# Expert stage of a hybrid block on one Trainium2 core: two 8 KB row gathers per pick become one 16 KB gather, and dots and sums run in the same turn

## The chip, the cores and the metric

The kernel runs on one core of a Trainium2 chip. The metric is the device time of one launch in microseconds (us), the median over several runs. One more execution was recorded by the hardware profiler; its trace is what the rows below come from.

## The reference, cut to what matters

A block of a hybrid model works on 256 tokens of width 2048 (with 256 context tokens for its recurrent branches): an RWKV-7 branch, a Mamba-2 branch, a merge, and last a feed-forward stage of experts (PEER). Only this last stage and the loads of its weights are touched by the change. All arrays are float32.

```
q = (tok @ wq).reshape(n, 8, 2, 128)                 # 8 heads, 2 half queries each
s = einsum('nhsd,hskd->nhsk', q, subkeys)            # scores against 128 keys per half
top_s, top_i = top_k(s, 16)
cand = top_s[:, :, 0, :, None] + top_s[:, :, 1, None, :]
best_s, best_j = top_k(cand.reshape(n, 8, 256), 16)
expert = i1 * 128 + i2                               # one of 16384 experts
gate = softmax(best_s)
act = gelu(einsum('nd,nhkd->nhk', x, u_tab[expert]))
out = einsum('nhk,nhkd->nd', gate * act, v_tab[expert])
x = x + g2x * rms_norm(out) * norm_post2
```

For each of the 256 tokens there are 8 heads with 16 experts each. Each expert costs a row of `peer_u` (2048 numbers, 8 KB), whose dot product with the token goes through a gelu, and a row of `peer_v` of the same size, which is added to the token's sum with the weight gate times gelu. That is 256 x 128 x 2 rows of 8 KB, 537 MB.

## The kernel before, in words

`hybrid_block` runs its stages one after the other: `rwkv`, `ssd`, and `tail`, which calls `mixing` (merge of the branches, `w_out`, the two norms) and `experts`. Each stage has one program per engine, written out in its order, and semaphores between them. The helper `Steps` counts named steps on one semaphore: `by(name, turn)` is the value after that step of that turn, `before(name, turn)` the one after the same step of the turn before.

Tokens lie on the 128 partitions, so 256 tokens are two tiles n = 0, 1. A **turn** is one head and one tile: 16 turns of 16 **picks**. One pick is one expert for each of the 128 tokens of the tile.

- `experts` first makes the queries on PE (`queries(h)`, L2448, 32 matmuls of 128x256 per head; `wq` comes in 2 MB pieces for one head, L1903, into the slot `w[:, 0]`) and the scores (`scoring(h)`, L2458). ACT copies both out of PSUM. Only when all eight heads are scored (`ready()` in `program`) does the loop over turns begin.
- DVE picks: `choose(i)` (L2259 to L2315, some 45 small instructions) finds the 16 best experts of head i for both tiles; `weigh(i)` (L2322 to L2326) makes the softmax gates after ACT's `exponent(i)` (L2386).
- GpSimd (POOL) gathers: `gather_u` (L2229) fetches 128 rows of 8 KB of `peer_u` into one of 4 buffers `ub`, `gather_v` (L2237) the same of `peer_v` into one of 4 buffers `vb`. A buffer is free again when the dot, or the matmuls, of the pick 4 earlier are done.
- DVE takes the dot (`dot`, L2334: one SCALAR_TENSOR_TENSOR of 128x2048 with a sum over the row) of each pick.
- After the 16 dots of a turn ACT takes one gelu (L2395), DVE multiplies by the gates (`coef`, L2356), ACT builds for each pick a diagonal matrix `diag` (L2401, 2 buffers), and PE adds diag times `vb` to the sums in PSUM (L2482: 4 matmuls of 128x512 per pick, 8 in the profile's count).
- So the two halves of a pick are a turn apart: `emit_v(v, ..., u, ...)` sums turn v while the dots of turn u = v + 1 are taken. POOL alternates strictly, one gather of v, one of u:

```
def emit_v(v, n, u, un, chosen):
    for k in range(TOPK):
        gather_v(v, n, k)
        if u is not None:
            gather_u(u, un, k)
```

- `choose` of the next head stands ahead of dot 4 in every other turn (`if k == 4 and chosen is not None`). DVE takes no dot while it runs.
- At the end, eight matmuls with zeros close the sums (L2489), ACT squares them (L2432), DVE scales and adds the residual (L2372 to L2379), and SP stores, tile 0 and then tile 1.

## Time and profile before

| what | us |
|---|---|
| median of 3 runs | 4236.61 (4233.58 to 4238.69) |
| the profiled execution | 4234.48 |
| its span, first to last instruction | 4232.7 |
| mean granted TensorE clock | 0.976 of full speed |
| PE busy | 3804.2 (90%) |
| DVE busy | 2031.0 (48%) |
| GpSimd busy | 778.2 (18%) |
| ACT busy | 729.5 (17%) |
| moved by DMA | 872.93 MB, 536.90 MB of them by the gathers |

The rows are read like this. Engines are PE (matmul), PEld (its weight load), DVE, ACT, POOL and SP; a group is named by its line of the kernel, and `out<-in` are its tensors. What stands in brackets or behind the last bar is the idle time of the engine just before, and what ended it. The share of busy time over the whole span mixes stages with different limits: the rwkv, ssd and mixing stages take the first 2790 us and are not touched.

### The profile page before, as it was taken

The page shows a single profiled execution, that of the slowest core. Times are in us where ns is not written, and L with a number is a line of the kernel's source. Part 1 is how long each engine was busy: PE and PEld are TensorE (multiplying, and loading weights), DVE is VectorE, ACT ScalarE, POOL GpSimd, SP SyncE. Part 2 cuts the span into 40 slices and gives each one's busy share as a digit, 9 for nine tenths or more (in the row PEclk, how much of TensorE's full clock was granted, in tenths as well). Part 3 has the DMA queues.
Part 4 walks back from the last instruction along what each step waited for, and adds up shares of the span by engine and source line. Part 5 has one row for each costly group of instructions (what it writes and reads, how often), then busy time and mean ns, then how long its engine had stood idle before and what let it go on. Part 6 is the DMA issues. An engine that isn't in the chain of part 4 may idle for free. (4 is left out here: it accounts for less than half of the span.)

```text
span 4232.7 us, 81256 instructions
## 1 busy us (share of the span) xinstructions
PE 3804.2 (90%) x35655; PEld 2313.7 (55%) x35655; DVE 2031.0 (48%) x3409; ACT 729.5 (17%) x1318; POOL 778.2 (18%) x755
## 2 busy tenths in 40 slices
PE   7999999999999989999999999988777777777777
PEld 3466666666666655666668888565223223322323
DVE  1355565556555547767770000035554554554541
ACT  2223222322233212221220000010110111111101
POOL 3000000001000100000010000004544444444431
PEclk9999999999999989999999999999999999999999
DMA  9211111111111117655663444437999999999996
GB/s 380 86 35 49 47 49 37 48 47 41 45 46 42 32 30 246 201 172 184 199 194 140 159 159 172 171 135 309 406 402 428 405 408 428 406 408 427 407 427 243
DMA packets 408824, 872.93 MB, mean 206 GB/s; under 512 B 16556, under 2 KB 250686, under 8 KB 341310
## 3 DMA queue, kind: packets, MB, share of 16 engines
q0 software_dynamic: 73728, 536.90, 30.5%
q1 hardware_dynamic: 243072, 284.82, 19.8%
q10 hardware_dynamic: 91710, 46.43, 3.8%
q8 instruction: 269, 4.41, 0.4%
q14 instruction: 45, 0.37, 0.0%
HBM read 863.87 MB, written 4.23 MB: 205 GB/s over the span
## 5 line engine op out<-in xcount | busy, mean ns | idle before, releaser
L2482 PE MATMUL ps<-w_slots,diag 128*128 128x512 f32 x2048 | 970.7, 622 | 302.6 <-DMA w_slots<-in_peer_v,ixv 264.5
L2482 PEld LDWEIGHTS ps<-w_slots,diag 128*128 128x128 f32 x2048 | 385.6, 197 | 887.5 <-issue 555.3
L979 PE MATMUL ps<-hT,w_slots 128*128 128x512 f32 (+1 forms) x1536 | 636.1, 542 | 3.1 <-PEq L230 2.2
L1719 PE MATMUL ps<-hT,w_slots 128*128 128x256 f32 (+1 forms) x1504 | 500.3, 486 | 6.5 <-PEq L655 4.9
L2334 DVE SCALAR_TENSOR_TENSOR junk<-w_slots,hT 128x2048 f32<-128x2048 f32 x128 | 293.4, 2292 | 290.3 <-DMA w_slots<-in_peer_u,ixu 289.6
L2334 DVE SCALAR_TENSOR_TENSOR junk<-ybT,hT 128x2048 f32<-128x2048 f32 x128 | 293.5, 2293 | 268.1 <-DMA ybT<-in_peer_u,ixu 266.3
L2237 POOL DMA_INDIRECT w_slots<-in_peer_v,ixv x256 | 293.7, 1147 | 550.0 <-PE ps L2482 497.3
L1719 PEld LDWEIGHTS ps<-hT,w_slots 128*128 128x128 f32 x1504 | 281.8, 191 | 173.3 <-issue 152.7
L979 PEld LDWEIGHTS ps<-hT,w_slots 128*128 128x128 f32 x1536 | 269.1, 191 | 179.7 <-issue 156.0
L2401 ACT ACTIVATE diag<-ident,coef 128x128 f32<-128x128 f32 x256 | 101.0, 400 | 1000.3 <-PE ps L2482 990.1
L695 POOL TENSOR_TENSOR bonus<-Kh 128x256 f32<-128x256 f32 x16 | 11.8, 735 | 1185.3 <-DVE Kh L916 1185.3
L2229 POOL DMA_INDIRECT ybT<-in_peer_u,ixu x128 | 170.1, 1329 | 196.2 <-PE ps L2482 81.5
L1603 DVE SCALAR_TENSOR_TENSOR w_slots<-w_slots,silu_c 128x512 f32<-128x512 f32 x240 | 193.9, 808 | 13.4 <-DVE w_slots L1603 0.9
L824 DVE SCALAR_TENSOR_TENSOR w_slots<-ps,em,w_slots 128x64 f32<-128x64 f32 x448 | 106.2, 278 | 195.0 <-PE ps L1078 195.0
L1986 PE MATMUL ps<-hT,w_slots 128*128 128x256 f32 x896 | 194.1, 379 | 0.3 <-PEq L1398 0.3
L1986 PEld LDWEIGHTS ps<-hT,w_slots 128*128 128x128 f32 x896 | 170.2, 190 | 23.8 <-issue 0.7
L844 DVE TENSOR_TENSOR w_slots<-ps,off 128x1024 f32<-128x1024 f32 x128 | 150.5, 1217 | 51.9 <-PE ps L1053 51.9
L2124 DVE TENSOR_TENSOR sga<-sga,ps 128x1024 f32<-128x1024 f32 x4 | 4.9, 1221 | 298.7 <-PE ps L1986 298.7
L2229 POOL DMA_INDIRECT w_slots<-in_peer_u,ixu x128 | 138.3, 1081 | 52.1 <-issue 42.7
L1078 PEld LDWEIGHTS ps<-w_slots 64*64 64x64 f32 x1792 | 71.1, 135 | 127.2 <-issue 109.4
L2448 PE MATMUL ps<-h2T,w_slots 128*128 128x256 f32 x512 | 115.7, 388 | 9.6 <-DMA w_slots<-in_peer_wq 8.4
L1439 POOL TENSOR_TENSOR xw<-xt,heads 128x256 f32<-128x256 f32 x48 | 27.7, 612 | 478.0 <-ACT xt L1498 478.0
(381 smaller groups left out, 4683.7 us busy)
## 6 DMA issues: line engine op xcount, KB each, us to landing
w_slots<-in_w_mod SPq DMA_DIRECT2D x128, 512.0 KB, 4.8
w_slots<-in_w_in SPq DMA_DIRECT2D x56, 1024.0 KB, 5.8
w_slots<-in_w_in ACTq DMA_DIRECT2D x44, 1024.0 KB, 6.9
w_mod_ring<-in_w_mod SPq DMA_DIRECT2D x16, 2048.0 KB, 12.6
w_slots<-in_w_in SPq DMA_DIRECT2D x7, 4096.0 KB, 13.8
w_slots<-in_w_branch_a SPq DMA_DIRECT2D x4, 4096.0 KB, 13.8
w_slots<-in_w_branch_b SPq DMA_DIRECT2D x4, 4096.0 KB, 13.8
w_slots<-in_w_out SPq DMA_DIRECT2D x4, 4096.0 KB, 12.7
```

The source lines that it names most:

```text
L824: stt(state(d, c), ps[:, 6, d * HEAD:(d + 1) * HEAD], em[:, z % 2, d, c:c + 1], state(d, c), ALU.mult, ALU.add).then_inc(*VD.did(f"c{j}_{d}"))
L844: tt(F[:, 2 * d:2 * d + 2, :, :], ps[:, 0:4, d * SEQ:(d + 1) * SEQ].rearrange("p r (h c) -> p h r c", h=2), off[:, l - 1, d, :].unsqueeze( ...
L979: last = mm(ps[:, 4, t0:TOK], w[m % 2][:, k, :], hT[:, k, t0:TOK], start=(k == 0), stop=(k == KC - 1))
L1603: stt(by_row[:, b, :], part, silu_c[:, k, 0:1], by_row[:, b, :], ALU.mult, ALU.add).then_inc(*VM.did(f"m{m}"))
L1719: last = mm(out, w[m % SLOTS_W][:, k, :], hT[:, k, t0:TOK], start=(k == 0), stop=(k == KC - 1))
L1986: last = mm(ps[:, bank + c // 2, (c % 2) * SEQ:(c % 2 + 1) * SEQ], slot[n][:, k, c * P:(c + 1) * P], rhs[:, k, :], start=(k == 0), stop=(k ...
L2229: nc.gpsimd.indirect_dma_start(ub[b], None, u_tab, bass.IndirectOffsetOnAxis(ap=ixu[:, n, k:k + 1], axis=0)).then_inc(u_in[b], 16)
L2237: nc.gpsimd.indirect_dma_start(vb[b], None, v_tab, bass.IndirectOffsetOnAxis(ap=ixv[:, n, k:k + 1], axis=0)).then_inc(v_in[b], 16)
L2334: nc.vector.scalar_tensor_tensor(junk[:, :], ub[k % NB], 1.0, h2_rows[:, n, :], ALU.mult, ALU.mult, accum_out=dots[:, k:k + 1]).then_inc(* ...
L2401: nc.scalar.activation(diag[:, k % 2, :], ident[:, :], ACT.Copy, scale=coef[:, k:k + 1]).then_inc(*DG.did(f"dg{k}"))
L2448: last = nc.tensor.matmul(ps[:, h % 2, s * SEQ:(s + 1) * SEQ], wq_at[h % 2][:, k, s * P:(s + 1) * P], h2T[:, k, :], start=(k == 0), stop=( ...
L2482: last = nc.tensor.matmul(ps[:, 4 * n + c, :], diag[:, k % 2, :], vb[k % NB][:, c * 512:(c + 1) * 512], start=False, stop=False)
```

## The change

1. The host lays `peer_u` and `peer_v` side by side in one table `peer_uv` whose rows have 4096 numbers, 16 KB. One gather per pick (L2222 of the new kernel) fetches both halves, 256 gathers of 128 rows in place of 512. There are 4 buffers `uv` of 16 KB per partition; they take the space of the 8 buffers of 8 KB.
2. Dots and sums belong to the same turn. For pick k DVE takes the dot, ACT the gelu of that one column, DVE builds the diagonal (`weighted`, one TENSOR_SCALAR of 128x128 with gelu and gate as its two scalars, 4 buffers), and PE runs the 4 matmuls. On DVE the diagonal of pick k - 1 stands behind the dot of pick k. The buffer is free when PE has done the pick (semaphore `x_pv`), and POOL waits for that before it issues the gather of pick k + 4.
3. `wq` is laid out by the host in 16 half heads, each contiguous, loaded as 1 MB pieces (`half_weights`). Heads 0 to 2 are done ahead of turn 0; eight half heads (heads 3 to 6) stand between the picks of turn 0 on PE, and head 7 behind it. The query banks move to PSUM 4 to 7, the sums of tile 0 have banks 0 to 3.
4. `choose` still stands ahead of dot 4 in the even turns; the gates of the head are made ahead of dot 8 of the same turn. The norm and store of tile 0 are done within the last turn.

```
-        ub = [part(spare, 0), part(spare, 1), part(w[:, 1, :], 2), part(w[:, 1, :], 3)]
-        vb = [part(w[:, 1, :], 0), part(w[:, 1, :], 1), part(w[:, 0, :], 0), part(w[:, 0, :], 1)]
+        uv = [flat(ybT), w[:, 1, 0:2 * D], w[:, 1, 2 * D:4 * D], w[:, 0, 0:2 * D]]
...
-        def program(emit_u, emit_v, engine, ready):
-            emit_u(0, 0)
-            ready()
-            with engine.Fori(0, PH - 1) as h:
-                emit_v(h * 2, 0, h * 2 + 1, 1, h + 1)
-                emit_v(h * 2 + 1, 1, h * 2 + 2, 0, None)
-            emit_v(TURNS - 2, 0, TURNS - 1, 1, None)
-            emit_v(TURNS - 1, 1, None, 0, None)
+        def program(turn, engine, after_first):
+            turn(0, 0, 1)
+            after_first()
+            turn(1, 1, None)
+            with engine.Fori(1, PH - 1) as h:
+                turn(h * 2, 0, h + 1)
+                turn(h * 2 + 1, 1, None)
+            turn(TURNS - 2, 0, None)
+            turn(TURNS - 1, 1, None)
... POOL
+                def turn(t_, n, chosen):
+                    wait_alone(pool, passed, *DU.before("ix", t_))
                     for k in range(TOPK):
-                        gather_v(v, n, k)
-                        if u is not None:
-                            gather_u(u, un, k)
+                        wait_alone(pool, passed, *(PV.by(f"v{k - NB}", t_) if k >= NB else PV.before(f"v{TOPK - NB + k}", t_)))
+                        nc.gpsimd.indirect_dma_start(uv[k % NB], None, uv_tab, bass.IndirectOffsetOnAxis(ap=ix[:, n, k:k + 1], axis=0)
+                                                     ).then_inc(uv_in[k % NB], 16)
... DVE
+                def weighted(t_, n, k):
+                    dve.wait_ge(*GE.by(f"g{k}", t_))
+                    dve.wait_ge(*(PV.by(f"v{k - NB}", t_) if k >= NB else PV.before(f"v{TOPK - NB + k}", t_)))
+                    if k == 0:
+                        dve.wait_ge(*DU.before("gt", t_))
+                    nc.vector.tensor_scalar(diag[:, k % NB, :], ident[:, :], acts[:, k:k + 1], gt[:, n, k:k + 1], ALU.mult,
+                                            ALU.mult).then_inc(*DG.did(f"dg{k}"))
+                def turn(t_, n, chosen):
+                    for k in range(TOPK):
+                        if k == 4 and chosen is not None:
+                            choose(chosen)
+                        if k == MID:
+                            if chosen is not None:
+                                weigh(chosen)
+                        dot(t_, n, k)
+                        if k:
+                            weighted(t_, n, k - 1)
+                        if final and k == MID + 2:
+                            normed(0)
+                    weighted(t_, n, TOPK - 1)
... PE
+                def turn(t_, n, chosen):
+                    for k in range(TOPK):
+                        pe.wait_ge(*DG.by(f"dg{k}", t_))
                         for c in range(4):
-                            last = nc.tensor.matmul(ps[:, 4 * n + c, :], diag[:, k % 2, :], vb[k % NB][:, c * 512:(c + 1) * 512],
+                            last = nc.tensor.matmul(ps[:, 4 * n + c, :], diag[:, k % NB, :], uv[k % NB][:, D + c * 512:D + (c + 1) * 512],
+                        if first and k % 2:
+                            m = 6 + k // 2
+                            half_query(m)
+                            if m % 2:
+                                scoring(m // 2 - 1)
```

What the written order makes of this is shown at three places. **DVE, two turns before the end, in the kernel before**: dots of one turn in a row (L2334), with nothing between them (`u_in` says that the gather of a `peer_u` row has landed).

```order
L2334 SCALAR_TENSOR_TENSOR junk,dots<-ybT,hT 128x2048 [waits x_du,u_in0]
L2334 SCALAR_TENSOR_TENSOR junk,dots<-ybT,hT 128x2048 [waits x_du,u_in1]
L2334 SCALAR_TENSOR_TENSOR junk,dots<-w_slots,hT 128x2048 [waits x_du,u_in2]
L2334 SCALAR_TENSOR_TENSOR junk,dots<-w_slots,hT 128x2048 [waits x_du,u_in3]
L2334 SCALAR_TENSOR_TENSOR junk,dots<-ybT,hT 128x2048 [waits x_du,u_in0]
```

**DVE at the same place in the changed kernel** (L2309 the dot, L2317 the diagonal; `uv_in` is the landing of a gather, `x_ge` the gelu, `x_pv` the matmuls of a pick).

```order
L2309 SCALAR_TENSOR_TENSOR junk,dots<-ybT,hT 128x2048 [waits x_du,uv_in0]
L2309 SCALAR_TENSOR_TENSOR junk,dots<-w_slots,hT 128x2048 [waits x_du,uv_in1]
L2317 TENSOR_SCALAR diag<-ident,acts,gt 128x128 [waits x_du,x_pv,x_ge]
L2309 SCALAR_TENSOR_TENSOR junk,dots<-w_slots,hT 128x2048 [waits x_du,uv_in2]
L2317 TENSOR_SCALAR diag<-ident,acts,gt 128x128 [waits x_pv,x_ge]
L2309 SCALAR_TENSOR_TENSOR junk,dots<-w_slots,hT 128x2048 [waits x_du,uv_in3]
L2317 TENSOR_SCALAR diag<-ident,acts,gt 128x128 [waits x_pv,x_ge]
```

The diagonal of pick 0 stands behind the dot of pick 1, which waits for the landing of gather 1, and so on. **PE in turn 0 of the changed kernel** (L2479 the sums of a pick, L2444 half a head of queries, L2458 scores).

```order
L2470 MATMUL ps<-g_rows,zero 128x512 x4
L2479 MATMUL ps<-ybT,diag 128x512 [waits x_dg]
L2479 MATMUL ps<-ybT,diag 128x512 x3
L2479 MATMUL ps<-w_slots,diag 128x512 [waits x_dg]
L2479 MATMUL ps<-w_slots,diag 128x512 x3
L2444 MATMUL ps<-h2T,w_slots 128x256 [waits q_cp,q_w0]
L2444 MATMUL ps<-h2T,w_slots 128x256 x15
L2479 MATMUL ps<-w_slots,diag 128x512 [waits x_dg]
L2479 MATMUL ps<-w_slots,diag 128x512 x3
```

Before, all 512 query matmuls (L2448) stood ahead of the first L2482; now the picks of turn 0 stand between those of heads 3 to 6. **POOL in the last turn**: the kernel before alternates the two gathers, each with its own semaphore; the changed one has one gather for a pick, which waits for PE alone.

```order
L2237 DMA w_slots<-in_peer_v,ixv 128x2048 [waits x_pv]
L2229 DMA ybT<-in_peer_u,ixu 128x2048 [waits x_du]
L2237 DMA w_slots<-in_peer_v,ixv 128x2048 [waits x_pv]
L2229 DMA w_slots<-in_peer_u,ixu 128x2048 [waits x_du]
```

```order
L2222 DMA ybT<-in_peer_uv,ix 128x4096 [waits x_pv]
L2222 DMA w_slots<-in_peer_uv,ix 128x4096 [waits x_pv] x3
```

A buffer of `u` used to come back with the dot (`x_du`); the joint buffer comes back with the matmuls (`x_pv`).

## Rows read from the trace of the kernel before

**Rows 1.** The page, the span in 40 slices: busy DMA in tenths, GB/s.
```profile
DMA  9211111111111117655663444437999999999996
GB/s 380 86 35 49 47 49 37 48 47 41 45 46 42 32 30 246 201 172 184 199 194 140 159 159 172 171 135 309 406 402 428 405 408 428 406 408 427 407 427 243
```

**Rows 2.** Stages: window, length, busy us (count) of five engines, PE clock, DMA share, GB/s.
```profile
2827.50:2925.30 97.80, 88.75 (x426) 77.82 (x425) 37.52 (x37) 10.44 (x16) 29.40 (x17) 0.95 0.70 271
2925.30:4147.50 1222.20, 919.65 (x1934) 363.13 (x1933) 663.75 (x987) 125.97 (x286) 561.52 (x484) 0.96 0.99 414
4147.50:4232.70 85.20, 63.76 (x144) 27.85 (x144) 9.62 (x6) 11.67 (x22) 11.24 (x12) 0.88 0.55 198
...
3400.00:3450.00 50.00, 37.42 (x82) 14.79 (x83) 28.91 (x74) 5.40 (x12) 20.02 (x19) 1.00 1.01 427
...
3165.00:3170.00 5.00, 3.77 (x9) 1.52 (x9) 2.30 (x2) 1.46 (x2) 2.41 (x2) 1.00 1.03 436
```

**Rows 3.** Timeline of PE, steady stretch: start us, us, line, count, idle before.
```profile
4122.23 3.67 PE L2482 MATMUL ps<-w_slots,diag 128*128 128x512 f32 x8 [1.19 <-DMA w_slots<-in_peer_v,ixv]
```

**Rows 4.** Timeline of POOL, the same stretch.
```profile
4126.72 0.96 POOL L2237 DMA_INDIRECT w_slots<-in_peer_v,ixv  x1 [2.66 <-PE ps L2482]
```

**Rows 5.** L2237 alone, 4147 to 4210 us, where the DMA queue is empty.
```profile
L2237 POOL DMA_INDIRECT w_slots<-in_peer_v,ixv x13: 936/936/962, 4146.3 to 4191.5; - x13
...
DMA to landing us min/median/max: 5.5/5.8/7.6
```

**Rows 6.** Timeline of DVE around one `choose` of the loop.
```profile
3102.13 2.29 DVE L2334 SCALAR_TENSOR_TENSOR junk<-ybT,hT 128x2048 f32<-128x2048 f32 x1 [2.63 <-DMA ybT<-in_peer_u,ixu]
...
3114.15 0.42 DVE L2259 COPY sc<-yaT 128x512 f32 x1
...
3129.98 2.29 DVE L2334 SCALAR_TENSOR_TENSOR junk<-ybT,hT 128x2048 f32<-128x2048 f32 x1 [0.21 <-DVE soft L2315]
3132.31 2.29 DVE L2334 SCALAR_TENSOR_TENSOR junk<-ybT,hT 128x2048 f32<-128x2048 f32 x1
...
3139.20 0.17 DVE L2346 COPY ixu<-idx 128x16 uint32 x1
```

**Rows 7.** Timeline of POOL beside the first dot of rows 6.
```profile
3103.26 1.97 POOL L2229 DMA_INDIRECT ybT<-in_peer_u,ixu  x1 [0.30 <-issue]
```

**Rows 8.** Timeline of PE behind three gaps.
```profile
3095.82 12.42 PE L2482 MATMUL ps<-w_slots,diag 128*128 128x512 f32 x24 [2.26 <-ACT diag L2401]
...
3143.93 5.44 PE L2482 MATMUL ps<-w_slots,diag 128*128 128x512 f32 x8 [6.32 <-DMA w_slots<-in_peer_v,ixv]
...
3155.00 3.67 PE L2482 MATMUL ps<-w_slots,diag 128*128 128x512 f32 x8 [1.61 <-DMA w_slots<-in_peer_v,ixv]
```

**Rows 9.** Windows (columns of rows 2) behind the gap that ends at 3095.82.
```profile
3096.40:3099.70 3.30, 3.30 (x5) 1.33 (x4) 2.30 (x2) 0.00 (x0) 0.26 (x1) 0.50 1.00 425
```

**Rows 10.** Chain that ended last, start of `experts`: start us, us, what.
```profile
2837.48 0.89 PE ps L2458 x8
2838.37 13.82 PE ps L2448 x64
```

**Rows 11.** Timeline of POOL: the first gather.
```profile
2827.50 1.23 POOL L2229 DMA_INDIRECT ybT<-in_peer_u,ixu  x1 [35.55 <-issue]
```

**Rows 12.** Chain that ended last, the end.
```profile
4147.51 56.90 PE ps L2482 x128
4204.41 6.88 PE ps L2489 x16
...
4211.39 1.97 ACT ybT L2432 x2
...
4219.91 3.81 DMA out_x<-w_slots
```

More of the change, by code:

```diff
@@ L2335, in dot @@
                                                    accum_out=dots[:, k:k + 1]).then_inc(*DU.did(f"dot{k}"))
-                def emit_u(u, n, chosen=None):
-                    fresh(DU)
-                    for k in range(TOPK):
-                        if k == 4 and chosen is not None:
-                            choose(chosen)
-                        if k == MID:
-                            if isinstance(u, int) and u == TURNS - 1:
-                                DU.skip("ixu")
-                            else:
-                                nc.vector.tensor_copy(ixu[:, 1 - n, :], idx[:, ds((u + 1) * TOPK, TOPK)]).then_inc(*DU.did("ixu"))
-                            wait_alone(dve, passed, *PV.before(f"v{TOPK - 1}", max(u - 1, 0) if isinstance(u, int) else u - 1))
-                            nc.vector.tensor_copy(ixv[:, n, :], idx[:, ds(u * TOPK, TOPK)]).then_inc(*DU.did("ixv"))
-                        dot(u, n, k)
@@ L2386, in exponent, with gelu @@
                     nc.scalar.activation(soft[:, :, :], soft[:, :, :], ACT.Exp).then_inc(*AC.did("exp"))
-                def emit_u(u, n):
-                    return
-                def emit_v(v, n, u, un, chosen):
+                def gelu(t_, k):
+                    act.wait_ge(*DU.by(f"dot{k}", t_))
+                    act.wait_ge(*DG.before(f"dg{k}", t_))
+                    nc.scalar.activation(acts[:, k:k + 1], dots[:, k:k + 1], ACT.Gelu).then_inc(*GE.did(f"g{k}"))
+                def turn(t_, n, chosen):
@@ L2392, in emit_v @@
                     fresh(GE)
-                    fresh(DG)
-                    act.wait_ge(*DU.by(f"dot{TOPK - 1}", v))
-                    nc.scalar.activation(acts[:, :], dots[:, :], ACT.Gelu).then_inc(*GE.did("gelu"))
-                    act.wait_ge(*DC.by("coef", v))
+                    first, final = (isinstance(t_, int) and t_ == at for at in (0, TURNS - 1))
                     for k in range(TOPK):
-                        if chosen is not None and k == 10:
+                        gelu(t_, k)
+                        if chosen is not None and k == 4:
@@ L2424, in _ @@
-                scoring(PH - 1)
-                program(emit_u, emit_v, act, lambda: None)
-                act.wait_ge(consts, 2)
-                act.wait_ge(*PV.by(f"v{TOPK - 1}", TURNS - 1))
-                act.wait_ge(opened, 2)
-                for n in range(2):
+                        if first and k in (5, 9, 13, 15):
+                            h = 3 + (5, 9, 13, 15).index(k)
+                            queries(h)
+                            scoring(h - 1)
+                        if final and k == 4:
+                            squared(0)
@@ L2464, in _ @@
                 queries(1)
[L2465 to L2482 removed]
+                queries(2)
@@ new lines, in _, with sums, turn @@
+                scoring(1)
+                def sums(m, first):
+                    for c in range(4):
+                        last = nc.tensor.matmul(ps[:, 4 * m + c, :], zero[:, :], g2_rows[:, c * 512:(c + 1) * 512], start=first, stop=not first)
+                    return last
+                def turn(t_, n, chosen):
+                    fresh(PV)
+                    first, final = (isinstance(t_, int) and t_ == at for at in (0, TURNS - 1))
+                    for k in range(TOPK):
+                        pe.wait_ge(*DG.by(f"dg{k}", t_))
+                        for c in range(4):
+                            last = nc.tensor.matmul(ps[:, 4 * n + c, :], diag[:, k % NB, :], uv[k % NB][:, D + c * 512:D + (c + 1) * 512],
@@ L2483, in emit_v @@
                                                     start=False, stop=False)
                         last.then_inc(*PV.did(f"v{k}"))
-                program(emit_u, emit_v, pe, lambda: None)
-                for m in range(2):
-                    for c in range(4):
-                        last = nc.tensor.matmul(ps[:, 4 * m + c, :], zero[:, :], g2_rows[:, c * 512:(c + 1) * 512], start=False, stop=True)
-                    last.then_inc(opened, 1)
+                        if first and k % 2:
[3 more added lines that the diff above has]
+                                scoring(m // 2 - 1)
@@ L2492, in _, with last_heads @@
+                        if final and k == 0:
+                            sums(0, False).then_inc(opened, 1)
+                def last_heads():
+                    queries(PH - 1)
+                    scoring(PH - 2)
+                    scoring(PH - 1)
+                    pe.wait_ge(scored, PH)
+                    sums(1, True)
+                sums(0, True)
+                program(turn, pe, last_heads)
+                sums(1, False).then_inc(opened, 1)
             @block.sync
             def _(sp):
-                for h in range(2, PH):
-                    sp.wait_ge(q_mm, h - 1)
-                    head_weights(sp, h)
+                for m in range(2, 2 * PH):
+                    sp.wait_ge(q_mm, m - 1)
+                    half_weights(sp, m)
```

202 lines of the change are left out of this document (91 added, 111 removed).

## The prediction

> **What bounds the kernel now.** I read the slices first: the DMA engines are at 9 tenths from slice 28 on, at 402 to 428 GB/s, and nowhere else for so long [rows 1]. The stages say the same [rows 2]: from 2925.3 to 4147.5 the DMA share is 0.99 while PE is busy 920 of 1222 us, DVE 664 and POOL 562. An undisturbed stretch moves 427 GB/s, so a gather of 128 x 8 KB (1.049 MB) takes 2.455 us and the pair for one pick 4.91 us. Of 537 MB that is 1257 us, and it does not get smaller with the change. What could be won lies around it: from 2827.5 to 2925.3 the share is only 0.70, and in the last 85.2 us it is 0.55 [rows 2], where 16 picks of the last turn run on PE alone in 56.9 us [rows 12].
>
> So the question is whether the new order still keeps the DMA engines full. Before, it does so with eight buffers, each held by one short piece of work. In the timeline of PE the matmuls of a pick take 3.67 us and wait for their gather [rows 3]; POOL starts the next gather 0.82 us after they end (4125.90 to 4126.72) [rows 4].
>
> **The change, term by term: the round of one buffer.** With four joint buffers, the gather of pick k + 4 waits for the matmuls of pick k, these for diagonal k, and this one stands on DVE behind the dot of pick k + 1, that is behind the landing of gather k + 1. From that landing:
> - dot k + 1: 2.33 us from one dot to the next instruction (3129.98 to 3132.31) [rows 6];
> - diagonal k, a new instruction: no row shows it; the bounds are 0.17 us (a copy of 128x16) and 0.42 us (a copy of 128x512) [rows 6]. I take 0.22, near the lower, since 128 columns are nearer to 16;
> - matmuls of pick k: 3.67, and 0.05 for the handover [rows 3];
> - POOL's start: 0.82 [rows 4];
> - issue to landing with an empty queue: 5.8 us for 1 MB [rows 5], plus 2.455 for the second megabyte: 8.25. The smallest of those rows, 5.5, gives 7.95; had the gather to be issued as two halves, another 0.94 would come on top (9.2).
>
> Sum: 15.3 us from landing k + 1 to landing k + 4, which is three picks. The DMA engines need 14.7. **The round is longer than the transfers**, so in every three picks the engines wait 0.6 us, and the pick costs 5.11 instead of 4.91. The gelu of one column, ACT's work, lies beside the next dot and costs nothing; if DVE caught up with it, it would show as a wait of 0.3. POOL issues half as many gathers, and it waits for PE in either kernel, so that saving is worth nothing.
>
> **The six chooses in the loop.** `choose` holds DVE for 15.8 us (3114.15 to 3129.98) [rows 6]. Before, the sums of the turn before went on beside it, and eight buffers were in flight. Now dot 4 and behind it diagonal 3 wait for it: matmuls 3 start at landing 3 + 2.33 + 15.8 + 2.33 + 0.27 = 20.7 instead of 5.1 + 2.6 = 7.7. The round starts again from there, so the whole 13 us are lost: 6 x 13 = 78 us (the seventh lies in turn 0). `weigh` and two copies (1 us) lie ahead of dot 8, in a round that has no slack, but only if DVE is late, which at 2.6 of 5.1 us it isn't.
>
> **Turn 0.** The first gather is issued at 2827.5 as now [rows 11]; nothing ahead of it is altered. Pick 1 lands at 2827.5 + 8.25 + 4.9 = 2840.7, diagonal 0 is there at 2843.3, and PE, behind the scores of head 1 (done at 2838.4 [rows 10]) and four zero matmuls of 0.86 [rows 12], at 2841.8. Then PE has 16 x 3.67 + ten half heads of 6.9 + six scores of 0.89 + 3.4 of zeros = 137 us [rows 10, 3], waits some 12 for diagonal 3 behind the first loop's `choose`, and 3 for handovers and a cold restart: turn 1 begins at 2995. The half heads are loaded beside it (1 MB each, 6.9 us of PE to hide it) and I cost them at nothing; uncovered, one costs up to 3 us. At 2995, 20 picks have landed.
>
> **Turns 1 to 15.** Matmuls 16 start at 2997; 239 picks later, 79.7 rounds of 15.3 = 1219 us and 78 us of chooses, less 5 because the last diagonal waits for no later dot and plus 2 for the norm of tile 0 inside the last turn: 4291. Then 3.7 of matmuls, 3.4 of zeros (half of 6.88), 8.5 from the square to the store of one tile (4211.4 to 4219.9) and 4.2 for the store [rows 12]: 4311.
>
> **The clock of PE.** Matmuls behind a gap of 2.26 us took 12.42 us for 24, 1.7 more than three picks in a row (56.9 / 16 = 3.56 each [rows 12]); behind one of 6.32 us, 5.44 instead of 3.67; behind one of 1.61 us, 3.67 [rows 8]. In the first case the granted clock is 0.50, 1.2 GHz, for 3.3 us [rows 9]. Three gathers land 4.91 apart and the fourth 5.5 or more, since the round is longer than they are: PE's gap ahead of it is 5.5 - 3.67 = 1.8 us, between the harmless and the costly row. But each `choose` leaves a gap of some 15 us. The matmuls behind it are slow by 1.75, that makes this buffer's round 17.05, the next gap 3.6, and that gap makes the next matmuls slow again: once fallen, the clock falls anew in each round. 80 rounds x 1.75 = 140 us, of which I take 126, as a round at a turn's end may escape. That gives 4311 + 126 = 4437, and with the 1.8 us between this execution's span and its time **4439 us**. The profiled execution took 4234.5, the median 4236.6, a difference of 2 that I add to nothing: I say **4440**.
>
> A bound for what is left out: POOL's issue next to a dot took 1.97 instead of 0.96 and ended 0.8 after the dot [rows 7, 6, 4]. If each round's late gather meets a dot, that is 0.6 x 80 = 48 us: 4488.
>
> The Trainium skill, DMA: Bandwidth & Descriptors, Anatomy of one DMA, gives about 2.0 us plus the bytes over 436 GB/s for a DMA from this queue, 4.4 us for 1 MB and 6.8 for 2. The trace says 5.8 for 1 MB, so the Trainium skill is low here, by 1.4 us; I go by the trace. By the Trainium skill the round would be 13.9 us.
>
> **The rivals.**
> - *The clock stays up* (or recovers between the chooses): the round is 15.3, 4311 + 2 = 4313; with POOL held by dots up to 4361. For it: gaps of 1.2 to 1.6 us never cost anything. Against: the chooses start the chain.
> - *The fetch is hidden*: if issue to landing of 2 MB is below 7.65 us, the DMA engines set the pace again, 239 x 4.91 = 1173 instead of 1219, and the gap ahead of every matmul is 1.2 us, as now [rows 3]: 4266. The smallest landing, 5.5 [rows 5], gives 7.95, so this is close. This is what the Trainium skill's 6.8 us (DMA: Bandwidth & Descriptors, Anatomy of one DMA) would make of it.
> - *Faster than before*: rows of 16 KB move at a higher rate. To break even, 239 picks and six chooses must fit into 4234.5 less what stands around them, which leaves 4.77 us per pick, 440 GB/s, with a round of 14.3; at 4.6 us (456 GB/s) the time is 4193. For it: half as many rows to start. Against: the best 5 us of the trace are at 436 GB/s [rows 2] with rows of 8 KB and the usual stretch at 427. The Trainium skill, DMA: Bandwidth & Descriptors, Where 436 GB/s comes from, puts the ceiling of the ports at 435 GB/s whatever the row; the trace agrees so far.
> - *Worse*: the clock falls in two of three picks, or POOL is held too and both delays add: 4440 + 126 = 4566.
>
> That the change doesn't do what it says is excluded by the order of the instructions shown above.
>
> **How the numbers follow.** Forecast 0.50, clock up 0.25, fetch hidden 0.09, worse 0.07, faster 0.07, and 0.02 for a tie between the last two kinds. A measurement of this kernel can tell about 0.2% from no change, 8 us; all cases but the last two lie over 30 us above. So faster 0.07, same 0.02, slower 0.91. The range takes in the first three cases and the bound by POOL: 4262 to 4490. The likeliest case alone: 4400 to 4490.
>
> **What would show it.** Right: turns without `choose` of 89 to 92 us and with it 13 more; DMA share about 0.85 in the loop; PE clock near 0.8 there, with a gap of over 3 us and slow matmuls once in three picks; DVE waiting for gathers, POOL for PE; PE on turn 1 at 2995 within 10; last landing to the end 23 us. If the DMA share between chooses is 0.95 and the clock near 1, it is the second case; 0.99, the third. It is wrong altogether if the gathers run above 436 GB/s, or if a `choose` costs less than 8 us.

## The result, and the profile after

The changed kernel takes 4490.45 us (median of 4 runs, 4485.32 to 4498.1), the kernel before 4236.94 in the same comparison: a ratio of 1.0613, 95% interval 1.0597 to 1.0628. The forecast was 4440, its range 4262 to 4490. The direction came true, and so did the main mechanism, a round of one buffer that is longer than its transfers; the price was 50 us short, and the time stands just outside the range. The profiled execution has a span of 4483.6 us.

The page, the span in 40 slices [rows 1]:

```profile
PEclk9999999999999999999999999998889888888988
DMA  9111111111111166566444452778879898898987
GB/s 383 57 45 47 43 46 45 46 46 45 47 35 44 28 222 200 166 188 201 151 169 152 156 203 89 301 292 327 345 320 361 320 348 329 314 357 332 350 344 295
```

Stages (windows; columns as in [rows 2]), from the first gather that POOL starts within turn 1 (2996.16) to the last landing, a steady stretch, the DMA gap behind one `choose`, and what is behind the last landing:

```profile
2996.20:4457.60 1461.40, 1002.65 (x1901) 399.10 (x1900) 701.98 (x1135) 69.34 (x259) 303.77 (x236) 0.87 0.86 340
3200.00:3600.00 400.00, 269.02 (x516) 107.31 (x516) 196.82 (x335) 18.77 (x71) 82.14 (x65) 0.88 0.86 338
...
3508.00:3521.00 13.00, 7.98 (x15) 3.52 (x16) 9.44 (x15) 3.40 (x6) 0.94 (x1) 0.66 0.01 3
...
4457.60:4483.60 26.00, 11.74 (x27) 4.67 (x25) 7.71 (x7) 3.75 (x5) 0.00 (x0) 0.85 0.10 40
```

Groups of instructions (busy us, mean ns | idle time before, and what ended it):

```profile
L2479 PE MATMUL ps<-w_slots,diag 128*128 128x512 f32 x1536 | 798.0, 673 | 349.4 <-DVE diag L2317 349.2
...
L2479 PE MATMUL ps<-ybT,diag 128*128 128x512 f32 x512 | 281.5, 701 | 126.9 <-DVE diag L2317 126.8
...
L2222 POOL DMA_INDIRECT w_slots<-in_peer_uv,ix x192 | 243.1, 1266 | 914.6 <-PE ps L2479 891.8
```

Where [rows 2] showed a DMA share of 0.99 at 414 GB/s for 1222 us, there are now 1461 us at 0.86 and 340. The sums agree: the last landing went from 4147.5 to 4457.6, 310 later; from there to the end stand 26.0 us instead of 85.2 [rows 2], 59 fewer; 251 is the difference of the two spans. So the change wins what it can at the end and loses five times as much in the loop.

The timeline shows the loop (start us, us, engine, line, what, idle before). A dot that waited for its gather marks the landing, to 0.05 us:

```profile
3602.85 2.29 DVE L2309 SCALAR_TENSOR_TENSOR junk<-ybT,hT 128x2048 f32<-128x2048 f32 x1 [4.03 <-DMA ybT<-in_peer_uv,ix]
...
3605.46 5.40 PE L2479 MATMUL ps<-w_slots,diag 128*128 128x512 f32 x8 [2.88 <-DVE diag L2317]
...
3608.89 2.29 DVE L2309 SCALAR_TENSOR_TENSOR junk<-w_slots,hT 128x2048 f32<-128x2048 f32 x1 [3.48 <-DMA w_slots<-in_peer_uv,ix]
...
3611.50 3.70 PE L2479 MATMUL ps<-ybT,diag 128*128 128x512 f32 x8 [0.64 <-DVE diag L2317]
...
3611.67 0.94 POOL L2222 DMA_INDIRECT w_slots<-in_peer_uv,ix  x1 [5.72 <-PE ps L2479]
...
3613.84 2.29 DVE L2309 SCALAR_TENSOR_TENSOR junk<-w_slots,hT 128x2048 f32<-128x2048 f32 x1 [2.39 <-DMA w_slots<-in_peer_uv,ix]
...
3616.01 0.94 POOL L2222 DMA_INDIRECT ybT<-in_peer_uv,ix  x1 [3.40 <-PE ps L2479]
...
3620.48 2.29 DVE L2309 SCALAR_TENSOR_TENSOR junk<-w_slots,hT 128x2048 f32<-128x2048 f32 x1 [4.08 <-DMA w_slots<-in_peer_uv,ix]
...
3620.96 2.62 POOL L2222 DMA_INDIRECT w_slots<-in_peer_uv,ix  x1 [4.01 <-PE ps L2479]
...
3625.85 2.29 DVE L2309 SCALAR_TENSOR_TENSOR junk<-ybT,hT 128x2048 f32<-128x2048 f32 x1 [2.66 <-DMA ybT<-in_peer_uv,ix]
...
3632.82 2.29 DVE L2309 SCALAR_TENSOR_TENSOR junk<-w_slots,hT 128x2048 f32<-128x2048 f32 x1 [4.41 <-DMA w_slots<-in_peer_uv,ix]
```

Follow one buffer. Landing k + 1 is at 3602.85, its dot and the diagonal release matmuls k at 3605.46 (slow, 5.40), POOL starts at 3611.67, landing k + 4 is at 3620.48: a round of 17.6. The next: 3608.89, 3611.50 (3.70), 3616.01, 3625.85: 17.0. The third: 3613.84, POOL at 3620.96 and held (2.62), 3632.82: 19.0. Three transfers need 14.6. Over all of turns 1 to 15 the median round is 17.9; 17.05 was forecast.

Two measures serve for all kernels below. **Turns**: the time from one copy of `ix` (L2346) to the next, for turns 2 to 14, with and without a `choose`. Here 106.3 and 94.1. (Where the chooses are spread, their second half and the load of gelu's table fall into the turns counted as without.) **Hold**: what the issues of turns 1 to 15 take over 0.94 us, summed. Here 83 us, 64 issues over 1.2.

### The profile page after: what moved, and what is told of

Same layout as the page of the kernel before. It is cut to its first block and busy times, and to the rows that moved or that the text cites. A ratio compares the mean times of both kernels' runs of the same rounds, so it can differ in the third digit from the quotient of the medians.

```text
span 4483.6 us, 80939 instructions
## 1 busy us (share of the span) xinstructions
PE 3897.1 (87%) x35655; PEld 2352.7 (52%) x35655; DVE 2095.7 (47%) x3649; ACT 671.8 (15%) x1298; POOL 500.8 (11%) x499
## 5 line engine op out<-in xcount | busy, mean ns | idle before, releaser
L2479 PE MATMUL ps<-w_slots,diag 128*128 128x512 f32 x1536 | 798.0, 673 | 349.4 <-DVE diag L2317 349.2
L2479 PEld LDWEIGHTS ps<-w_slots,diag 128*128 128x128 f32 x1536 | 318.0, 214 | 823.4 <-DVE diag L2317 461.8
L2309 DVE SCALAR_TENSOR_TENSOR junk<-w_slots,hT 128x2048 f32<-128x2048 f32 x192 | 440.1, 2292 | 624.6 <-DMA w_slots<-in_peer_uv,ix 624.5
L2479 PE MATMUL ps<-ybT,diag 128*128 128x512 f32 x512 | 281.5, 701 | 126.9 <-DVE diag L2317 126.8
L2222 POOL DMA_INDIRECT w_slots<-in_peer_uv,ix x192 | 243.1, 1266 | 914.6 <-PE ps L2479 891.8
L2377 ACT ACTIVATE acts<-dots 128x1 f32<-128x1 f32 x256 | 51.9, 203 | 1478.3 <-DVE junk L2309 1478.2
L2479 PEld LDWEIGHTS ps<-ybT,diag 128*128 128x128 f32 x512 | 110.2, 224 | 293.3 <-DVE diag L2317 168.4
L2309 DVE SCALAR_TENSOR_TENSOR junk<-ybT,hT 128x2048 f32<-128x2048 f32 x64 | 146.7, 2293 | 235.6 <-DMA ybT<-in_peer_uv,ix 189.4
L695 POOL TENSOR_TENSOR bonus<-Kh 128x256 f32<-128x256 f32 x16 | 11.7, 734 | 1182.0 <-DVE Kh L916 1182.0
L2222 POOL DMA_INDIRECT ybT<-in_peer_uv,ix x64 | 81.6, 1275 | 425.4 <-PE ps L2479 387.2
L2444 PE MATMUL ps<-h2T,w_slots 128*128 128x256 f32 x512 | 114.4, 383 | 2.0 <-POOL x_eps L2216 1.2
## 6 DMA issues: line engine op xcount, KB each, us to landing
w_slots<-in_w_in SPq DMA_DIRECT2D x7, 4096.0 KB, 13.6
w_slots<-in_w_branch_b SPq DMA_DIRECT2D x4, 4096.0 KB, 13.6
```

Source lines behind the costliest of these rows:

```text
L2222: nc.gpsimd.indirect_dma_start(uv[k % NB], None, uv_tab, bass.IndirectOffsetOnAxis(ap=ix[:, n, k:k + 1], axis=0)).then_inc(uv_in[k % NB], 16)
L2309: nc.vector.scalar_tensor_tensor(junk[:, :], uv[k % NB][:, 0:D], 1.0, h2_rows[:, n, :], ALU.mult, ALU.mult, accum_out=dots[:, k:k + 1]).th ...
L2377: nc.scalar.activation(acts[:, k:k + 1], dots[:, k:k + 1], ACT.Gelu).then_inc(*GE.did(f"g{k}"))
L2444: last = nc.tensor.matmul(ps[:, 4 + h % 2, s * SEQ:(s + 1) * SEQ], wq_at[s][:, k, :], h2T[:, k, :], start=(k == 0), stop=(k == KC - 1))
L2479: last = nc.tensor.matmul(ps[:, 4 * n + c, :], diag[:, k % NB, :], uv[k % NB][:, D + c * 512:D + (c + 1) * 512], start=False, stop=False)
```

## The experiments

All are edits of the changed kernel unless said otherwise.

| kernel | us | ratio to before (95%) | turns with / without choose | hold | clock, 3200 to 3600 |
|---|---|---|---|---|---|
| changed kernel | 4490 | 1.0613 (1.0597 to 1.0628) | 106.3 / 94.1 | 83 | 0.88 |
| diagonal behind its dot | 4273 | 1.0097 (1.0080 to 1.0114) | 90.0 / 81.8 | 22 | 0.90 |
| no chooses | 4433 | 1.0458 (1.0425 to 1.0491) | - / 95.2 | 62 | 0.86 |
| zeros behind each pick | 4511 | 1.0652 (1.0635 to 1.0670) | 106.7 / 96.7 | 134 | 0.94 |
| quarter dots | 4358 | 1.0308 (1.0283 to 1.0333) | 98.4 / 84.2 | 11 | 0.90 |
| two gathers of 8 KB rows | 4338 | 1.0252 (1.0214 to 1.0291) | 97.7 / 83.3 | 114 | 0.88 |
| dots in halves | 4474 | 1.0581 (1.0546 to 1.0616) | 105.8 / 91.7 | 26 | 0.86 |
| zeros beside the dot, 512 columns | 4590 | 1.0845 (1.0826 to 1.0863) | 120.1 / 96.2 | 11 | 1.00 |
| those, and dots in halves | 4584 | 1.0822 (1.0804 to 1.0840) | 119.7 / 96.3 | 11 | 1.00 |
| zeros beside the dot, 256 columns | 4464 | 1.0540 (1.0510 to 1.0570) | 104.1 / 93.2 | 134 | 1.00 |
| those, and dots in halves | 4453 | 1.0533 (1.0508 to 1.0558) | 103.2 / 91.7 | 82 | 1.00 |
| chooses spread | 4191 | 0.9899 (0.9867 to 0.9931) | 82.7 / 78.8 | 25 | 0.94 |
| gelu's table early | 4188 | 0.9897 (0.9881 to 0.9914) | 82.9 / 77.1 | 12 | 0.96 |
| that, and dots in halves | 4193 | 0.9904 (0.9888 to 0.9921) | 83.1 / 77.4 | 8 | 0.97 |

**The diagonal behind its own dot.**

```diff
                         dot(t_, n, k)
-                        if k:
-                            weighted(t_, n, k - 1)
+                        weighted(t_, n, k)
...
-                    weighted(t_, n, TOPK - 1)
```

> Edit: diagonal k stands on DVE right behind dot k, not behind dot k + 1; four buffers, 16 KB rows and chooses as they are. Theory R (the round of a buffer is longer than its transfers): the round now spans four picks, and from landing k to landing k + 4 stand 2.3 of dot, 0.4 of waiting for the gelu, 0.3 of diagonal, 3.7 of matmuls, 0.8 of POOL and 8.3 of fetch, 15.8 us against 19.6 of transfers. The DMA engines set the pace (4.91 per pick, 1159 us for the 236 picks behind turn 0) and only a part of each choose is left (about 8 us, since four gathers are in flight when it begins): 2996 + 1159 + 48 + 30 = 4233, so 4210 to 4270, PE's clock near 1. Rival S (rows of 16 KB move more slowly in this loop, 345 GB/s, and the pick costs 6.1 us in any order): above 4440, no gain beyond the chooses.

4273 us, 3 above the range expected. One instruction moved by one pick gives back 217 of the 254 us. Windows and timeline:

```profile
3200.00:3600.00 400.00, 281.38 (x576) 112.38 (x576) 235.10 (x417) 19.98 (x77) 79.67 (x73) 0.90 0.92 387
```

```profile
3636.27 3.70 PE L2477 MATMUL ps<-w_slots,diag 128*128 128x512 f32 x8 [1.15 <-DVE diag L2317]
...
3640.78 0.94 POOL L2222 DMA_INDIRECT w_slots<-in_peer_uv,ix  x1 [3.91 <-DVE junk L2309]
...
3641.11 3.70 PE L2477 MATMUL ps<-ybT,diag 128*128 128x512 f32 x8 [1.14 <-DVE diag L2317]
...
3645.62 0.94 POOL L2222 DMA_INDIRECT ybT<-in_peer_uv,ix  x1 [3.91 <-PE ps L2477]
...
3645.95 3.70 PE L2477 MATMUL ps<-w_slots,diag 128*128 128x512 f32 x8 [1.14 <-DVE diag L2317]
```

The matmuls start every 4.84 us at full clock, 2.097 MB / 4.84 = 433 GB/s. So rows of 16 KB reach the full rate (theory S falls), and a round that spans four transfers is hidden. What is left are the chooses, 90.0 against 81.8.

**No chooses.** `turn(h * 2, 0, h + 1)` becomes `turn(h * 2, 0, None)`, and the copies read head 1's picks. It leaves out the choice of heads 2 to 7.

> Edit: the six chooses in the loop, with their exp and weigh, are left out; turns 2 to 15 read head 1's picks and gates again. Everything else as in the changed kernel. Theory R: the six chooses cost 13 to 15 us each, so 78 to 90 less, 4400 to 4412, if the clock falls without them too. Rival C (only the 15 us gap behind a choose starts the chain of slow matmuls): the granted clock is near 1 in the whole loop and about 130 us more are gone, 4270 to 4290.

4433 us, 21 above the range expected. Its turns take 95.2 and its clock is 0.86. The even and the odd turns differ here without any choose, 96.5 against 94.1. So a choose costs 9.8 us (106.3 against the 96.5 of the same turns), not 13 to 15, and rival C falls: the clock drops without them.

**Zeros behind each pick.**

```diff
                         last.then_inc(*PV.did(f"v{k}"))
+                        if not (isinstance(t_, int) and t_ in (0, TURNS - 1)):
+                            for _ in range(16 if chosen is not None and k == 2 else 1):
+                                nc.tensor.matmul(ps[:, 4 * n, :], zero[:, :], g2_rows[:, 0:512], start=False, stop=False)
```

> Edit: PE does one matmul of zeros into the sums behind every pick of turns 1 to 14 (0.43 to 0.86 us, in what was a gap of 1.2 to 3 us), and 16 of them behind pick 2 of the turns with a choose. Theory R with the clock on the path: the granted clock stays near 1 between the chooses, the 133 us that PE's matmuls are longer than 256 x 3.70 (798.0 + 281.5 against 947) go, most of them on the path: 4360 to 4400. Rival P (POOL held by the dots and the fetch itself make the round, the slow matmuls lie beside it): under 30 us less, 4460 to 4490, with the clock near 1.

4511 us, slower than the changed kernel, with the clock at 0.94. It settled nothing: a matmul of zeros (0.86 us) stands ahead of the next pick when that one is ready, and the hold rose from 83 to 134.

**Quarter dots.** The dot takes `0:D // 4`; three quarters of u are not multiplied.

> Edit: each dot takes 512 of the 2048 columns (the other three quarters of u are fetched and not used), about 0.65 us instead of 2.3. Theory R: the round is 1.65 shorter (13.6 against 14.7 of transfers) and POOL is held for a shorter time, so the DMA engines set the pace between the chooses: 4.91 per pick and 6 x 13: 4250 to 4320, clock near 1 between the chooses. Rival S (16 KB rows are slow in themselves): above 4440. Should the time lie between 4330 and 4400, the dot was only its own length on the path (80 x 1.65 = 132) and the fetch of 10.1 us is real.

4358 us, the third case of the expectation, 132 less. But the turns without a choose are at 84.2 where transfers alone would be 16 x 4.84 = 77.5: a round of 13.6 us by the forecast's sum should have been hidden, and was not. Here the term for the fetch first looked too small.

**Two gathers of 8 KB rows.**

```diff
-                        nc.gpsimd.indirect_dma_start(uv[k % NB], None, uv_tab, ...).then_inc(uv_in[k % NB], 16)
+                        nc.gpsimd.indirect_dma_start(uv[k % NB][:, 0:D], None, u_tab, ...).then_inc(uv_in[k % NB], 16)
+                        nc.gpsimd.indirect_dma_start(uv[k % NB][:, D:2 * D], None, v_tab, ...).then_inc(v_in[k % NB], 16)
```

PE also waits for `v_in`.

> Edit: only the joint table is taken back. In the changed kernel's order, POOL starts two gathers of 8 KB rows per pick (u, then v, both behind the matmuls that free the buffer), the dot waits for u alone. Theory R: the dot of a late pick starts 2.4 us earlier and the round of three picks is 2.33 + 0.3 + 0.05 + 3.7 + 0.8 + 5.8 = 13.0 with POOL free and up to 15 with POOL held, against 14.7 of transfers: between the chooses near 4.91 per pick, six chooses of 13: 4280 to 4340. Rival F (it is the number of buffers and the order alone; a gather's bytes arrive in the same time however they are cut, and 0.94 of POOL comes on top): 4470 to 4520.

4338 us: the joint table by itself costs 152 of the 254. The dot needs only u, and a joint gather makes it wait for v too; how much of the 152 this is, and how much the single fetch of twice the size, no run separates.

**Dots in halves.** Two instructions of 1024 columns; the first sum is the gelu's bias.

> Edit: each dot is two instructions of 1024 columns (the first sum enters as the gelu's bias), so that the time for which one DVE instruction can hold POOL's DMA issue is halved; DVE's work per pick grows by about 0.1 us. The order is that of the changed kernel. Theory H (POOL is held by the dot it meets, 83 us in the loop, and this is on the path of the round): the excess of the issues over 0.94 falls to 30 to 50 us and the time by as much, less 8 for the longer dots: 4450 to 4465. Rival N (the hold is beside the path): 4485 to 4500, whatever the excess. Third: POOL is held as long as DVE has two-operand work queued, with no gap between the halves: excess still 80, 4490 to 4500.

4474 us. The group of POOL's issues:

```profile
L2223 POOL DMA_INDIRECT w_slots<-in_peer_uv,ix x192 | 198.3, 1033 | 903.2 <-PE ps L2482 890.6
```

1033 ns instead of 1266; the hold fell from 83 to 26, the time by 16, and the intervals of the two ratios overlap. The hold is real, but most of it is not on the path; the result stands between theory H and rival N.

**Zeros beside the dot**, so that they are over before the diagonal is there.

```diff
+                            pe.wait_ge(uv_in[(k + 2) % NB], t_ * (16 * TOPK // NB) + 16 * ((k + 2) // NB + 1))
+                            for _ in range(30 if chosen is not None and k == 2 else 3):
+                                nc.tensor.matmul(ps[:, 4 * n, :], zero[:, :], g2_rows[:, 0:512], start=False, stop=False)
```

> Edit, on the changed kernel: behind the matmuls of pick k, PE waits for the landing of pick k + 2 and then does three matmuls of zeros into the sums (1.3 us at full clock), beside the dot that the next diagonal waits for; 30 of them in the turns with a choose at its place. Nothing else; turns 0 and 15 are as they were. Theory K (the half clock behind the gaps is on the path, about 1.75 us in most of the 80 rounds, 133 us of extra PE time in the changed kernel): the granted clock of the loop rises from 0.87 to 0.97 or more and the turns without a choose go from 94 to 85 to 88 us: 4360 to 4400. Rival P (the slow matmuls lie beside the fetch): the clock rises as much and the time stays at 4470 to 4495.

4590 us: my mistake in the length. A matmul of 512 columns in f32 is recorded as two and takes 0.86 at full clock, so three take 2.6 and a pick 6.0. The window shows PE without a gap:

```profile
3200.00:3600.00 400.00, 400.00 (x933) 177.09 (x933) 182.02 (x317) 17.55 (x65) 55.30 (x59) 1.00 0.81 309
```

> Edit: the zeros beside the dot and the dots in halves together. If clock and hold are two separate pieces of one round, their gains add: the half dots gave 16 us over the changed kernel, so this kernel is 10 to 25 us below the one with the zeros alone, and its turns without a choose are near the forecast's round with neither delay, 16 x 15.3 / 3 = 82 us. If the zeros themselves stand in the way, or the hold is another size at full clock, the difference is outside 5 to 40 us.

4584 us, for the same reason; neither says anything of the question. With 256 columns each:

> Edit: as the zeros beside the dot, but each of 256 columns, not 512: the three of one pick take 1.3 us (before this they took 2.6, and PE with 6.0 us per pick became the bound), the 30 in a turn with a choose 12.9. They fit into the 2.6 us between a landing and its diagonal. Theory K (the half clock is on the path): granted clock in the loop 0.95 or more, turns without a choose 85 to 90 us instead of 94, 4370 to 4430. Rival P (it lies beside the path): the clock rises and the turns stay at 93 to 95, 4470 to 4500.

4464 us. Windows, and timeline (one PE row, then POOL and the dots):

```profile
3200.00:3600.00 400.00, 350.91 (x1019) 187.03 (x1018) 198.14 (x335) 18.77 (x71) 101.99 (x65) 1.00 0.87 341
```

```profile
3651.19 2.29 DVE L2309 SCALAR_TENSOR_TENSOR junk<-w_slots,hT 128x2048 f32<-128x2048 f32 x1 [2.84 <-DMA w_slots<-in_peer_uv,ix]
...
3653.80 3.70 PE L2479 MATMUL ps<-w_slots,diag 128*128 128x512 f32 x8 [0.40 <-DVE diag L2317]
...
3658.31 2.52 POOL L2222 DMA_INDIRECT w_slots<-in_peer_uv,ix  x1 [4.02 <-PE ps L2479]
...
3663.46 2.29 DVE L2309 SCALAR_TENSOR_TENSOR junk<-ybT,hT 128x2048 f32<-128x2048 f32 x1 [2.58 <-DMA ybT<-in_peer_uv,ix]
...
3670.79 2.29 DVE L2309 SCALAR_TENSOR_TENSOR junk<-w_slots,hT 128x2048 f32<-128x2048 f32 x1 [5.03 <-DMA w_slots<-in_peer_uv,ix]
```

This run comes nearest to an answer. The clock is 1.00, the matmuls take 3.70, and the median round is still 17.9. From landing to POOL's start are 7.1 us (3651.19 to 3658.31), as forecast; from there to the landing 12.5, though the last gather had landed at 3663.46. Rival P is nearer: the clock gave 26 us by the medians, 31 by the ratios, not 126. As the hold rose to 134 meanwhile, those 26 are the net of the two, and the time lies in neither of the ranges expected.

> Edit: those zeros and the dots in halves together. If clock and hold are separate pieces of the round, their gains add: turns without a choose near 82 to 85 (16 x 15.3 / 3 = 82 is the forecast's round without either), 15 to 40 us below the kernel with the zeros alone. If one of the two only fills what the other leaves: within 10 us of it.

4453 us, 11 less, and the intervals of the two overlap. The hold is 82, as in the changed kernel, and the clock 1.00; the turns without a choose are at 91.7, as they were with a hold of 26 and a clock of 0.86, and not at 82. Against the changed kernel, with the same hold, the clock is worth 37 us here (34 by the ratios). Whether the two gains add stays open, since no run had both delays gone at once. But neither of them alone holds most of the loss.

**The fetch, read from all traces.** For each gather of turns 1 to 15 I took the *lead*, from POOL's start to the landing of the gather before it, and the time from that landing to its own (number of gathers: median fetch from POOL's start, median interval, us). Intervals under 4.5 or over 11 us, dots that waited for DVE or stood behind a `choose`, are left out. Issues are under 1.1 us unless "held" is said:

| lead, us | changed kernel | no chooses | zeros, 256 columns | diagonal behind its dot |
|---|---|---|---|---|
| -1 to 1 | 15: 8.1, 7.3 | 33: 8.2, 7.4 | 2: 8.1, 7.4 | 4: 8.1, 7.9 |
| 1 to 3 | 34: 8.2, 6.6 | 21: 8.3, 6.9 | 5: 8.2, 6.7 | - |
| 3 to 4 | 11: 10.3, 6.6 | 6: 10.4, 6.8 | 27: 9.3, 6.0 | - |
| 3 to 4, held | 4: 10.5, 6.7 | 2: 9.8, 6.6 | 43: 8.8, 5.5 | - |
| 4 to 5 | 42: 9.6, 4.9 | 46: 9.6, 4.9 | 4: 9.6, 4.9 | 3: 10.0, 5.5 |
| 4 to 5, held | 31: 10.9, 6.2 | 14: 11.2, 6.7 | 41: 11.1, 6.7 | 4: 10.1, 5.6 |
| 5 to 6 | 23: 10.1, 4.8 | 39: 10.1, 4.8 | 22: 10.9, 5.2 | 7: 10.1, 4.8 |
| 5 to 6, held | 26: 11.3, 5.8 | 13: 10.9, 5.5 | 61: 11.0, 5.4 | 1: 11.5, 6.2 |
| 6 to 8 | 17: 11.7, 4.9 | 36: 11.5, 4.9 | 5: 11.4, 5.0 | 156: 11.9, 4.9 |

The four kernels give nearly one curve. A gather into an empty queue takes 8.1 us. If that were all, a lead of 8.1 - 4.84 = 3.3 us would be enough to follow the one before at 4.84. In these four it is not: at a lead of 3 to 4 the fetch takes 8.8 to 10.5 and the interval is 5.5 to 6.8; it needs over 4 us with POOL free and over 6 with POOL held. The median lead is 4.7 in the changed kernel, 4.8 in the one with zeros, and 7.0 with the diagonal behind its dot. But a short lead is not the cause by itself: in the two runs with zeros of 512 columns 16 gathers stand at a lead of 3 to 4 with POOL free, and in the median they take 8.1 to 8.2 us and land 4.8 to 4.9 behind the one before.

**When each DMA engine was done.** The packets of the traces show what differs. Each gather has 144 of them: 128 rows of 16 KB, and 16 packets of 4 bytes, which I read as the mark that each of the 16 DMA engines sets behind its rows. The gather of 3658.31 in the timeline above has 15 of its 16 marks between 8.6 and 10.0 us after POOL's start, and the last at 12.1. Counted over the gathers as in the table above, with POOL held or free:

| kernel | gathers | of these, last engine over 1 us behind the median engine |
|---|---|---|
| changed kernel | 205 | 88 |
| no chooses | 232 | 58 |
| zeros, 256 columns | 209 | 147 (131 of them with only one or two engines late) |
| zeros, 512 columns | 199 | 19 (23 with the dots in halves) |
| diagonal behind its dot | 187 | 76 |

With zeros of 256 columns and a lead of 4 to 6, the 20 gathers without a late engine take 10.1 us and land 4.9 behind the one before, the 108 with one take 11.0 and land 5.5 behind. To weigh this, take for each gather the later of two times: 8.1 us (and its hold) from POOL's start, or 4.85 behind the one before. In the run with zeros of 256 columns the intervals up to 11 us, 231 of them, are in sum 195 us longer than that, and only 8 of the 195 lie in the 68 gathers whose last engine is within 1 us of the median; in the changed kernel it is 129, and 17 of them in 134 such gathers of 231. So what the fetch takes beyond the forecast's sum is the wait for the last one or few of 16 engines. At a lead of 7 us they do no harm: with the diagonal behind its dot the gathers land 4.85 apart in the median all the same. Why an engine falls behind no run shows.

**A version that beats both.** Diagonal behind its dot, and `choose` made a generator with 13 pieces:

```diff
+                    pieces = choose(chosen) if chosen is not None else None
                     for k in range(TOPK):
...
                         dot(t_, n, k)
-                        if k:
-                            weighted(t_, n, k - 1)
+                        weighted(t_, n, k)
+                        if k >= 1 and pieces is not None and k < TOPK - 1:
+                            next(pieces, None)
```

> Edit: diagonal k behind dot k, and each choose cut into 13 pieces of 0.8 to 1.5 us that stand on DVE behind the diagonals of picks 1 to 13 (exp behind gelu 15, weigh behind diagonal 15). Theory R: DVE's 2.3 + 0.4 + 0.35 + 1.5 = 4.6 us per pick stays below the 4.85 of a transfer, so turns with a choose take the 80 us of those without, 10 less than in the run with the diagonal alone moved (90.5 against 80.4): 4273 - 60 = 4213, so 4200 to 4225, below the kernel before by 0.3 to 0.8 per cent. Rival D (a DVE that is busy 95 per cent of a pick falls behind its landings, and its pieces hold POOL): turns of 83 to 86, 4235 to 4260.

4191 us, 1.0% below the kernel before (0.7 to 1.3) and 9 below the range expected. The kernel before with its chooses spread was not run, so how much of the 1.0% the new order gives, and how much the spreading, stays open. Windows and timeline, at the end of a turn with a choose:

```profile
3200.00:3600.00 400.00, 307.75 (x629) 121.96 (x628) 254.78 (x442) 21.61 (x85) 83.78 (x79) 0.94 0.98 413
```

```profile
3605.24 0.23 ACT L2387 ACTIVATE soft<-soft 128x32 f32<-128x32 f32 x1
...
3609.60 1.28 ACT L2392 ACT_TABLE_LOAD   x1 [4.13 <-DVE junk L2323]
...
3610.90 0.20 ACT L2392 ACTIVATE acts<-dots 128x1 f32<-128x1 f32 x1
...
3611.31 0.35 DVE L2331 TENSOR_SCALAR diag<-ident,acts,gt 128x128 f32<-128x128 f32 x1 [1.81 <-ACT acts L2392]
...
3611.72 6.50 PE L2494 MATMUL ps<-ybT,diag 128*128 128x512 f32 x8 [3.65 <-DVE diag L2331]
```

Behind exp the table of gelu has to come back, 1.28 us, and it comes when the diagonal is waiting. Loading it at once, by one gelu into a spare tile behind exp:

> Edit, on the kernel with the chooses spread (4191): ACT does one gelu of a column into a spare tile right behind each exp, so that the table of gelu is loaded there (1.28 us) and not in front of the first pick of the next turn, where its gelu came 1.5 us late and PE's gap was 3.65 with a slow pick behind it. Theory T (these seven loads are on the path and start the slow clock): turns with a choose fall from 82.7 towards 79, 10 to 25 us less: 4166 to 4181. Rival B (four buffers in flight cover 1.3 us): 4184 to 4196.

4188 us: the turns without a choose, in which these loads stood, went from 78.8 to 77.1, but the times are the same within their spread. Rival B.

> Edit: as the kernel with gelu's table loaded early, and each dot in two instructions of 1024 columns. POOL was held for 25 us in this loop; of that 15 to 20 go, DVE has 0.1 to 0.2 more per pick. If the hold is on the path here: 5 to 15 us below the kernel without it. If the buffers cover it: the same within 4, or up to 10 slower because DVE has less slack next to the pieces of choose.

4193 us: no difference; with a lead of 7 us the buffers cover what hold is left.

## Why the prediction was right or wrong

- **A round longer than its transfers**: right, and the cause. Moving one diagonal makes it four transfers long and gives 217 us back.
- **Dot, diagonal, handover, matmuls, POOL's start, 7.09 us**: right, 7.12 measured (3608.89 to 3616.01). Also a transfer: 4.84 against 4.91.
- **Issue to landing 8.25**: this is the step that failed. It is right for what I took it from, an empty queue (8.1 to 8.2 measured), and I used it where the queue isn't empty. The round is three gathers deep, so POOL starts a gather 3 to 5 us ahead of the landing before it, and there the fetch takes 9.3 to 11. The median over turns 1 to 15 is 10.1. At full clock the sum is then 7.1 + 10.6 = 17.7 (the fetches of the run with zeros of 256 columns), against 17.9 measured. Part of these 10 us the forecast had as transfers: at a lead of 4.7 a gather that lands 4.85 behind the one before has taken 9.55. What it put at nothing is that a gather has landed only when the last of its 16 DMA engines is done, and that one or a few of them often end 1 to 3 us late. With the clock at 1.00 the kernel takes 4464 where the sum without the clock's term says 4313; these 151 us are left for that wait and the hold.
- **PE's clock, 126 us**: the size in PE's own time is right. Its matmuls took 798.0 and, from the other buffer, 281.5 us; less 256 x 3.70 that is 132 more. But I added that time to the path in full, and that is the second step that failed: the runs give 26 to 37 for it. Nor do the chooses start it: without them the clock is 0.86. Two errors of opposite sign, this one and the fetch, left a sum that was only 50 off; that the number came so near was luck.
- **POOL held, bound 48**: the issues are held for 83 us, and about 16 of it show in the time. By the arithmetic 4488 was the nearest number to 4490; by its reason it was not. Its 0.6 us per round stands on no row either: the row it names shows 1.97 against 0.96, which is 1.0 more, and 80 of those are 80 us, a bound of 4520.
- **Chooses, 6 x 13**: right as a mechanism, 12 to 21 us too dear. The DMA engines stand for 13 us (3508 to 3521), and turns with one take 12.2 more than those without. But 2.4 of these stand there without a choose too (96.5 against 94.1), so one costs 9.8, and leaving all six out saves 57 to 66 us.
- **Turn 0**: the first gather came at 2821.5, not 2827.5, and the first matmuls of turn 1 at 2991.7, against 2997. **Tail**: 26 us, against 23.
- **The rivals.** *The clock stays up* was priced at 4313 to 4361; with the clock at 1.00 the kernel takes 4464, so this case missed by 100 us, for the same fetch. *The fetch is hidden*: no. The Trainium skill's fit (DMA: Bandwidth & Descriptors, Anatomy of one DMA), 6.8 us for 2 MB, is 1.3 below the shortest usual fetch here, and says nothing of one that starts beside another. *Faster*: the rate is 433 GB/s at best, not over 436. *Worse*, 4566: both delays were there, and the time is 76 us below the sum.
- **The signs**: turns of 89 to 92 were foretold, 94.1 came; 13 more with a choose, 12.2; DMA share 0.85, 0.86; clock 0.8, 0.87; the gap of over 3 us once in three picks was one of 2.9 to 3.3 at changing places.

## What to carry to other kernels

The latency of a DMA in an empty queue is a lower bound for one that is issued while another runs. Take from the trace, for gathers at several leads, how long after the one before they land and when each DMA engine was done, and ask of a new order what lead it leaves: the wait is for the last engine, and it was hidden here at a median lead of 7.0 us and not at 4.7. A lag of one step between producer and consumer costs a whole buffer of that lead: with four joint buffers it took the round from four transfers to three. And what a slow engine costs on its own clock is not what the path pays: 132 us more of PE were worth 26 to 37.
